# A four-layer hybrid stack on one core: x multiplied unscaled in the feed-forward stages, its transposes moved between the last row products, a shorter triangular inverse

## The reference, cut to what matters

```python
def rmsnorm(x, gain):
    y = x * lax.rsqrt(jnp.mean(x * x, axis=-1, keepdims=True) + 1e-6)
    return y * gain

def swiglu(h, w_in, w_out):                       # w_in (1024, 2*2816), w_out (2816, 1024)
    gate, up = jnp.split(h @ w_in, 2, axis=-1)
    return (jax.nn.silu(gate) * up) @ w_out

for l in range(2):                                # first block
    x = x + 0.5 * swiglu(rmsnorm(x, ffn1_norm[l]), ffn1_w_in[l], ffn1_w_out[l])
    x = x + hybrid_mixer(rmsnorm(x, mix_norm[l]), ...)
    x = x + 0.5 * swiglu(rmsnorm(x, ffn2_norm[l]), ffn2_w_in[l], ffn2_w_out[l])
for l in range(2):                                # second block
    x = x + mixer_2(rms_norm(x, g_mix[l]), ...)
    x = x + square(relu(rms_norm(x, g_ffn[l]) @ w_up[l])) @ w_down[l]   # w_up (1024, 4096)
return rms_norm(x, g_final)
```

## Time and profile before

| | |
|---|---|
| median of 3 runs | 2430.78 us (2430.58 to 2431.09) |
| the profiled execution | 2430.55 us, its span 2428.7 us |
| mean granted TensorE clock | 0.992 |
| PE busy | 2378.2 us, 98% of the span |
| DVE, ACT, POOL busy | 1549.4 (64%), 1388.8 (57%), 145.2 (6%) |
| HBM | 386.6 MB moved, 159 GB/s |

### The profile page before, as it was taken

The page is one execution under the profiler, slowest core; times in us unless marked ns, Lnnn a source line. Parts: engine busy times, 40 slices in busy tenths (PEclk is TensorE's granted clock), DMA queues, the critical chain, the costliest instruction groups (busy, mean ns, idle before and its releaser), DMA issues. The chain is left out here.

```text
span 2428.7 us, 40849 instructions
## 1 busy us (share of the span) xinstructions
PE 2378.2 (98%) x17221; PEld 2239.4 (92%) x17221; DVE 1549.4 (64%) x1891; ACT 1388.8 (57%) x1872; POOL 145.2 (6%) x119
## 2 busy tenths in 40 slices
PE   7999999999999999999999999999999999999998
PEld 7998999998999999899999899899989989998998
DVE  5555678756655655667865655559785554978545
ACT  5455788265554545678725555546854444685444
POOL 0000012100000000001300000000030000004000
PEclk9999999999999999999999999999999999999999
DMA  7554544224655555444414455544545555454553
GB/s 230 192 186 144 161 139 132 88 88 156 208 175 190 174 191 178 154 144 137 137 53 139 158 193 187 190 137 133 155 158 191 187 183 154 123 155 166 193 189 122
DMA packets 312310, 386.58 MB, mean 159 GB/s; under 512 B 10796, under 2 KB 287296, under 8 KB 312128
## 3 DMA queue, kind: packets, MB, share of 16 engines
q1 hardware_dynamic: 311848, 383.87, 48.6%
q10 hardware_dynamic: 280, 0.10, 0.0%
HBM read 382.89 MB, written 1.06 MB: 158 GB/s over the span
## 5 line engine op out<-in xcount | busy, mean ns | idle before, releaser
L275 PE MATMUL bank<-xhi,whi 128*128 128x256 f32 x3712 | 1066.7, 287 | 5.4 <-ACT xhi L383 3.4
L276 PE MATMUL bank<-xlo,whi 128*128 128x256 f32 x3712 | 1054.9, 284 | 0.0
L277 PE MATMUL bank<-xhi,wlo 128*128 128x256 f32 x3712 | 1054.8, 284 | 0.0
L267 DVE TENSOR_TENSOR wlo<-raw,whi 128x2048 fp32r<-128x2048 f32 x360 | 831.2, 2311 | 337.9 <-ACT whi L252 333.9
L252 ACT ACTIVATE whi<-raw 128x2048 fp32r<-128x2048 f32 x351 | 669.0, 1907 | 232.1 <-PE bank L277 225.4
L275 PEld LDWEIGHTS bank<-xhi,whi 128*128 128x128 f32 x3712 | 717.0, 193 | 11.6 <-issue 5.0
L276 PEld LDWEIGHTS bank<-xlo,whi 128*128 128x128 f32 x3712 | 717.0, 193 | 4.7 <-issue 1.9
L277 PEld LDWEIGHTS bank<-xhi,wlo 128*128 128x128 f32 x3712 | 716.6, 193 | 0.0
L275 PE MATMUL bank<-whi,yhi 128*128 128x512 f32 x608 | 237.5, 391 | 0.0
L276 PE MATMUL bank<-wlo,yhi 128*128 128x512 f32 x608 | 237.4, 390 | 0.0
L277 PE MATMUL bank<-whi,ylo 128*128 128x512 f32 x608 | 236.5, 389 | 0.0
(11 more groups left out here) (381 smaller groups left out, 2914.6 us busy)
## 6 DMA issues: line engine op xcount, KB each, us to landing
raw<-in_w_in SPq DMA_DIRECT2D x92, 1024.0 KB, 5.2
raw<-in_ffn_w_in SPq DMA_DIRECT2D x88, 1024.0 KB, 5.1
raw<-in_ffn_w_out SPq DMA_DIRECT2D x44, 1024.0 KB, 4.9
raw<-in_w_gate SPq DMA_DIRECT2D x32, 1024.0 KB, 5.5
raw<-in_w_up SPq DMA_DIRECT2D x32, 1024.0 KB, 5.4
raw<-in_w_down SPq DMA_DIRECT2D x32, 1024.0 KB, 4.9
raw<-in_w_branch_b SPq DMA_DIRECT2D x8, 1024.0 KB, 5.1
raw<-in_w_branch_a SPq DMA_DIRECT2D x8, 1024.0 KB, 5.2
```

Of the source, the lines that this page charges most:

```text
L267: e.tensor_tensor(wlo[s][:], raw[s][:], whi[s][:].bitcast(F32), ALU.subtract).then_inc(lo_done[s], 1)
L275: e.matmul(o, ahi, bhi, start=start, stop=False, skip_group_check=True)
L276: e.matmul(o, ahi, blo, start=False, stop=False, skip_group_check=True)
L277: return e.matmul(o, alo, bhi, start=False, stop=stop, skip_group_check=True)
```

## The change

1. Feed-forward stages (borders in `LATE_AT`: 0, 2, 3, 5, 7, 9) no longer scale x by rstd before the product. x itself is transposed, with the gain in xhi and xlo; rstd is put on a diagonal by ACT, spread over all partitions by one matmul with ones (`spread_pe`), copied by ACT (`spread_act`), and each gate and up result is multiplied by it per token: ffn1 gets two more DVE operations a block, ffn2 one operation with another operand.
2. At these borders `last_rows` runs its parts in another order, with the transposes of x by token half and column half between them (`turn_half`); the last quarter is transposed inside the first product (`late_first_product`). DVE's and ACT's norm work is ordered by column half.
3. In the delta part, POOL writes the masked blocks by column (`M_columns`); T's product at levels 4 and 5 is replaced by a transpose of U copied by ACT; level 6 works on 64 columns only.
4. The other borders keep their way; counters of semaphores are renumbered.

```diff
+        def late_first_product(e, n, o, j):
+            s, _ = n
+            def part(b, chunks):
+                for c in chunks:
+                    if b == 0:
+                        chunk_ready(e, j, c)
+                    mm = product3(...)
+                return mm
+            split_ready(e, n)
+            part(0, range(4))
+            turn_half(e, j, 1, 1)
+            part(1, range(4))
+            part(0, range(4, KC))
+            part(1, range(4, KC)).then_inc(multiplied[s], 1)
+
+        def turn_half(e, j, t, h):
+            if h and t:
+                e.wait_ge(x_new, j + 1)
+            else:
+                e.wait_ge(x_part, late(j) * 3 + (2 * h + t + 1))
+            for c in range(4 * h, 4 * h + 4):
+                late_bank = h and c == KC - 1
+                if late_bank and not t:
+                    continue
+                for u in (0, 1) if late_bank else (t,):
+                    mm = e.transpose(tq[c][:, u * P:(u + 1) * P], x[:, u, c * P:(c + 1) * P], ident)
+                if t:
+                    mm.then_inc(xt_done, 1)
+
+        def spread_pe(e, j):
+            e.wait_ge(late_norm, late(j) * 5 + DIAG_READY)
+            e.matmul(bank[1][:, 0:T], ones, diag, start=True, stop=True).then_inc(spread_product, 1)
...
+        def last_rows(e, n1, a1, n2, a2, ready2, j):
             split_ready(e, n1)
+            if j in LATE_AT:
+                row_part(e, n1, *a1, 0, 0)
+                row_part(e, n1, *a1, 1, 0)
+                row_part(e, n1, *a1, 0, 1)
+                ready2()
+                split_ready(e, n2)
+                row_part(e, n2, *a2, 0, 0, stop=True).then_inc(half_rows, 1)
+                row_part(e, n2, *a2, 1, 0, stop=True).then_inc(half_rows, 1)
+                row_part(e, n1, *a1, 1, 1).then_inc(multiplied[n1[0]], 1)
+                turn_half(e, j, 0, 0)
+                row_part(e, n2, *a2, 0, 1, stop=True).then_inc(half_rows, 1)
+                turn_half(e, j, 1, 0)
+                row_part(e, n2, *a2, 1, 1, stop=True).then_inc(multiplied[n2[0]], 1)
+                turn_half(e, j, 0, 1)
+                return
...
+        def late_border_dve(e, n, scale, j):
+            s, r = n
+            for k, (t, h) in enumerate(((0, 0), (1, 0), (0, 1))):
+                e.wait_ge(half_rows, (late(j) - 1) * 3 + (k + 1))
+                add_part(e, t, h, scale).then_inc(x_part, 1)
+            late_lo_dve(e, j, range(4))
+            e.wait_ge(multiplied[s], r + 1)
+            add_part(e, 1, 1, scale).then_inc(x_new, 1)
...
+        def late_dve(e, j, second):
+            split_lo_half(e, second, 0)
+            late_lo_dve(e, j, range(4, KC))
+            split_lo_half(e, second, 1)
+        def late_act(e, j, second):
+            split_hi(e, second)
+            late_hi_act(e, j, range(4))
+            late_square_act(e, j)
+            late_hi_act(e, j, range(4, KC))
+            late_scale_act(e, j)                 # Ln, Exp, two copies of ident scaled by rstd
...
         def ffn1_act(e, l, r0, u0, j, f):
             if first:
-                rstd_act(e, j)
+                late_square_act(e, j)
                 split_hi(e, unit(r0, u0))
                 e.wait_ge(cols_done, 1)
-                xhi_act(e, j, gain)
+                late_hi_act(e, j, range(KC))
                 split_hi(e, unit(r0, u0 + 1))
+                late_scale_act(e, j)
...
+            def scale_gate(i):                   # DVE, first in block i
+                e.wait_ge(multiplied[s], r + 1)
+                if i == 0:
+                    e.wait_ge(spread_done, late(j) + 1)
+                e.tensor_tensor(two(gbuf), two(gate_of(i)[:]), spread_two(), ALU.mult).then_inc(gate_dve, 1)
...
-                e.tensor_tensor(hbuf, hbuf, up_bank(i)[:], ALU.mult).then_inc(h_done, 1)
+                e.tensor_tensor(hbuf, hbuf, up_bank(i)[:], ALU.mult).then_inc(gate_dve, 1)
+                e.wait_ge(gate_dve, n * 3 + UP_GATED)
+                e.tensor_tensor(two(hbuf), two(hbuf), spread_two(), ALU.mult).then_inc(h_done, 1)
...
             for i in range(FF1_BLOCKS):
+                scale_gate(i)
                 if i:
                     split_lo(e, unit(r0, u0 + 3 * i + 1))
                 log_sigmoid_of_gate(i)
...
-                mm = e.matmul(bank[0][:, c * BLK:(c + 1) * BLK], M_blocks[:, :, c], const("row_of"), ...)
+                mm = e.matmul(bank[0][:, c * BLK:(c + 1) * BLK], M_columns[:, c, :], const("row_of"), ...)
...
+                last = s == LEVELS - 1           # U times L, and T times M, at the last level:
+                            mm = e.matmul(b4(g)[0:64, i, 64:P], Lb[g][:, i, 0:64], Ub[g][:, i, 64:P], ...)
+                            mm = e.matmul(b4(g)[0:64, i, 0:64], Tb[g][:, i, 0:64], Mb[g][:, i, 64:P], ...)
-                            mm = e.matmul(halves(b4(4 + g)[:, i, 0:64], s, False), Mb[g][:, i, :],
-                                          halves(Tb[g][:, i, :], s, True)[:, :, 0, :], start=True, stop=True)
+                if not last:
+                    for g in range(GROUPS):
+                        e.wait_ge(*V["tu_done"](l, (s - LOW + 1) * 4 + g))
+                        for i in range(4):
+                            mm = e.transpose(b4(4 + g)[:, i, :], Ub[g][:, i, :], ident)
+                        mm.then_inc(V["t_turned"].sem, 1)
...
+            for k in range(2 * GROUPS):          # ACT
+                e.wait_ge(*V["t_turned"](l, k))
+                e.activation(flat(Tb[k % GROUPS]), bank[4 + k % GROUPS][:], ACT.Copy).then_inc(V["t_level"].sem, 1)
...
-                e.tensor_tensor(Mb[g], Lb[g], const("below")...to_broadcast([P, 4, P]), ALU.mult)   # POOL
+                e.tensor_tensor(M_columns[:, :, g * 32:(g + 1) * 32].rearrange("p c (i k) -> p i k c", i=4),
+                                Lb[g].rearrange("p i (k c) -> p i k c", c=BLK), ..., ALU.mult)
```

More of the change, by code:

```diff
@@ L235, in col, with late, normed, late_gain @@
             return cols[:, bass.ds(i, 1)] if not isinstance(i, int) else cols[:, i:i + 1]
+        LATE = (("ffn1_norm", 0), ("mix", 0), ("ffn2_norm", 0), ("ffn1_norm", 1), ("mix", 1), ("ffn2_norm", 1),
+                ("mix", 0), ("g_ffn_2", 0), ("mix", 1), ("g_ffn_2", 1), ("final", 0))
+        LATE_AT = [j for j in range(len(LATE)) if LATE[j][0] in COL]
+        NORMED_AT = [j for j in range(len(LATE)) if j not in LATE_AT]
+        ABS, EXP, LN, SIGMOID = 1, 2, 3, 4
+        SCALED, LOG_SIGMOID, UP_GATED = 1, 2, 3
+        SQUARED, LOG_TAKEN, SCALE_READY, DIAG_READY = 2, 3, 4, 5
+        def late(j):
+            return LATE_AT.index(j)
+        def normed(j):
+            return NORMED_AT.index(j)
+        def late_gain(j, c):
+            return col(*LATE[j], c)
         def unit(r0, u, i=0):
@@ new lines, in late_hi_act, with late_square_act @@
+        def late_hi_act(e, j, chunks):
+            for c in chunks:
+                e.wait_ge(xt_done, j * KC + (c + 1))
+                e.activation(xhi[:, c, :], tq[c], ACT.Copy, scale=late_gain(j, c)).then_inc(xhi_done, 1)
+        def late_square_act(e, j):
+            d = late(j)
+            e.wait_ge(x_part, d * 3 + 3)
+            e.activation(xn[:, 0, :], x[:, 0, :], ACT.Square, accum_out=sumsq[:, 0:1]).then_inc(late_norm, 1)
+            e.wait_ge(x_new, j + 1)
+            e.activation(xn[:, 1, :], x[:, 1, :], ACT.Square, accum_out=sumsq[:, 1:2]).then_inc(late_norm, 1)
@@ new lines, in late_scale_act @@
+        def late_scale_act(e, j):
+            d = late(j)
+            e.wait_ge(late_norm, d * 5 + SQUARED)
+            e.activation(lnv[:], sumsq[:, 0:2], ACT.Ln, bias=eps, scale=1.0 / D).then_inc(late_norm, 1)
+            e.wait_ge(late_norm, d * 5 + LOG_TAKEN)
+            e.activation(rstd[:], lnv[:], ACT.Exp, scale=-0.5).then_inc(late_norm, 1)
+            e.wait_ge(late_norm, d * 5 + SCALE_READY)
+            e.activation(diag[:, 0:P], ident, ACT.Copy, scale=rstd[:, 0:1])
+            e.activation(diag[:, P:T], ident, ACT.Copy, scale=rstd[:, 1:2]).then_inc(late_norm, 1)
@@ L475, in ffn1_pe @@
             first = l == 0 and u0 == 0
-            norm_pe(e, j, first)
+            if first:
+                turn_half(e, j, 0, 0)
+                turn_half(e, j, 1, 0)
+                turn_half(e, j, 0, 1)
             def gate_up(i):
@@ L2289, in ffn2_pe @@
                     e.wait_ge(*W["relu"](l, i - 2))
-                feature_product(e, up_unit(r0, u0, i), gate_of(i), xhi, xlo, j if i == 0 else None)
                 if i:
+                    feature_product(e, up_unit(r0, u0, i), gate_of(i), xhi, xlo)
                     h_ready(i - 1)
+                else:
+                    late_first_product(e, up_unit(r0, u0, i), gate_of(i), j)
+                    spread_pe(e, j)
+                if i == 1:
+                    e.wait_ge(spread_done, late(j) + 1)
                 if 0 < i < BLOCKS2 - 1:
@@ L2333, in relu @@
                     e.wait_ge(*W["square"](l, i - 1))
```

(5 more changed lines are left out.)

195 lines of the change are left out of this document (122 added, 73 removed).

## The result

The changed kernel takes 2407.91 us (median of 4 runs, 2406.05 to 2410.98) against 2430.94 us for the kernel before on the same chip (2430.58 to 2432.66): a ratio of 0.9905 [0.989, 0.992], 23.0 us faster. The forecast was 2404.3 us with a range of 2396 to 2415. The profiled execution after took 2406.55 us with a span of 2404.7; the span before was 2428.7, so the two traces differ by 24.0 us.

| term | predicted us | measured us |
|---|---|---|
| gather (its first instruction to L1300, after: L1467), two layers | -9.4 | -5.6 |
| levels, two layers | -13.0 | -15.0 |
| borders 2, 3, 5, 7, 9, without the clock | -9.2 | -11.4 |
| clock at borders 7 and 9 | -3.0 | -3.0 |
| clock elsewhere, with one wait that it had hidden before | +1.3 | +2.7 |

A forecast was written before the change was run, and what follows sets the result against it. PE, busy 98%, bounds the kernel, so gains must be PE work, idle time or clock. Terms -9.4, -13.0, -9.2, -3.0, +1.3, +2.8, +4.1 sum to -26.4 us: forecast 2404.3, range 2396 to 2415.

The forecast's parts named there:

- gather: Inverse in the delta part: contiguous loads let L1300 start 4.7 us earlier per layer, -9.4 us for two.
- levels: Inverse's three levels: T by transposes and a 64-column last level take 22.7 instead of 29.20 us, -13.0 for two layers.
- borders 2, 3, 5, 7, 9: Stage borders: transposes and spread cost PE 2.45 us instead of 4.29, 1.85 saved at each, -9.2 us.
- clock at borders 7 and 9: The two half-clock stretches after late borders vanish, 1.5 us each, -3.0 us.
- clock elsewhere: The four unchanged borders shift in time and may lose clock: 4 x 2/9 x 1.5 = +1.3 us.
- last blocks: Last block of each ffn1 stage: later split of h stalls PE 0.7 us, four times, +2.8 us.
- so 448.9: Time DVE's chain behind the gather ends; PE, ready at 447.1, waits 1.8 us before L1300.
- Rival 1: Last level: the 64-column loads give nothing, 3.2 us less gain per layer, 2410.7 us; chance 0.12.
- Rival 4: Borders: nothing removed, since xlo 4 to 7 or the diagonal come late; +9.2 us, 2413.5; chance 0.08.
- First stage: First feed-forward stage: up(0) starts 1.85 us later, rows(0) another 2.25; +4.1 us (2 to 6).
- Rivals 2: Gather: POOL's column writes are dear and the gather starts late; 2410.1 us; chance 0.12.
- rival 3: ffn1: the gate's scale delays each down unit's split, so 40 row products start late; slower, 2440 us; chance 0.04.

The follow-up runs named there:

- all_three: The changed kernel plus the edits of first_stage, last_block and pool_later together; 2395.33 us, ratio 0.9849 to the kernel before.
- split_behind: all_three with DVE's weight split between the spread and the copies before L1300 moved behind the levels; 2396.39 us, ratio 0.9856 to the kernel before.
- pool_later: The changed kernel with POOL's four q products held until DVE has spread the inverted blocks; 2406.40 us, ratio 0.9890 to the kernel before.
- last_level: The kernel before with only the last level on 64 columns, T's products kept; 2429.29 us, ratio 0.9987.
- last_block: The changed kernel, token scale before the wait for up; in ffn1's last blocks, sigmoid and gate product before the last unit's split; 2408.23 us, ratio 0.9898.
- first_stage: The changed kernel with the first stage's last transposes ahead of its first product and `setup_dve` two blocks later; 2406.60 us, ratio 0.9891 to the kernel before.

## Why the prediction was right, and where it was off

**The sum.** It came within 2.4 us of the traces' 24.0, and that is partly luck: the gather's 3.8 us, and 1.4 and 1.1 us of clock and last blocks, were lost against 4.2 us more from levels and borders.

**Gather: the mis-sized term.** Forecast 4.7 us a layer, measured 2.83 and 2.81. The part on PE's read was right: loads at 192 ns. The 3.8 us for the gather was a little high, since 3.79 / 32 took a row that runs to its modelled end: at full clock the gather takes 3.5 us to the product behind it (all_three), and with the clock falling inside it 4.05 and 4.42 after. The failing step was "The two feature products behind it take 14.27 x 0.80 = 11.4 us at full clock". They took 14.10 us at 0.80 again. The text had allowed for one fall worth 1.5 us, "inside that wait". The fall here cost 14.10 x 0.20 = 2.8 us, and the wait of 1.8 couldn't hide it: 0.83 us of it is ACT's copy of PE's own last transposes, which moves with PE and stands there after as well (`[0.83 <-ACT arena L1581]`; split_behind shows the same 0.8 with DVE out of the way). Only 1.0 was left as cover, 1.8 us went through, and 4.7 - 1.8 = 2.9 is what was measured. So the clock by itself is enough for the miss.

The rows show why half-clock time fell from 10.2 to 6.8 us in each of these stretches and the products gained nothing: before, 4.5 and 4.2 us of it lay on the gather, whose strided loads take 310 ns at either level, so the clock cost nothing there. After, 5.7 and 4.9 us lie on the products, not much less than the 5.7 and 6.0 of before, and the rest slows the contiguous gather too.

The second step, DVE's chain "so 448.9", was wrong too, hidden behind the first: it left out what POOL does to it. (Its own terms, with the overlaps that it names taken off, end at 448.4; with POOL away L1300's place comes at 18.61 us in all_three, 448.6 in the times of the trace before.) With the gather 3 us earlier, the steps begin while POOL's q products run. Before, these ended at 437.17 and the steps began at 437.49 (434.36 + 2.81, trace of before); after, they ran from 437.94 to 442.97 and the steps from 441.36. Of POOL's 5.03 us, 2 are what it loses under DVE's weight split in either kernel. pool_later and all_three show that with both costs absent the stretch is 18.6 to 18.8 us, a gain of 5.0, and the stretches of 20.0 to 20.65 us show that taking the clock's cost away alone gives back only 0.2 to 1.0: the forecast's mechanism and its sum hold under its own two assumptions.

The Trainium skill (SBUF — State Buffer, on who interferes with whom) says that a DVE instruction with two SBUF inputs contends with a GpSimd instruction that reads SBUF. The trace agrees: 1.02 us for a 0.43 us step beside POOL's products, and 2.77 us for a product of 0.73 under DVE's split. The prediction had the rows of both engines at hand, and did not put the two timelines beside each other at their new times.

**Levels: right, a little low.** 7.44 and 7.56 us a layer against 6.5. No wait came ("So nothing waits"). The last level runs at 0.060 us a step against the 0.062 worked out from the earlier trace rows. The two numbers agree by some luck, as the 0.118 it started from is 0.112 from start to start. About half of the surplus is in the last level (3.87 us instead of 4.3, without the 0.3 us hand-over that was set aside), the other half in the two levels ahead of it (17.9 us instead of 18.4). The recorded bounds don't fit each other: gains of 3.3 to 7.5 us belong to levels of 21.7 to 25.9 us, not 18.4 to 25.9. Rival 1 (64-column loads give nothing) is refuted by the step of 0.060 us. last_level adds what the prediction didn't see: without T's edit that cheaper level would have bought 1.9 us instead of 3.5.

**Borders: right, a little low.** -2.36, -2.37, -2.37, -2.18 and -2.16 us instead of 1.85 each (the half-clock stretches, 1.5 each, apart). The tight cover of 0.2 us for xlo held: there is no wait for L432 at any late border. About half of what is more than 1.85 comes from the first product itself: before, it followed its eight xlo chunk by chunk, and its 48 matmuls took 6.03 us where 48 x 0.12 = 5.76 is the pace. Those gaps of under 0.1 us are in no wait list. The rest is that transposes and spread take 2.2 us and not 2.45 (4.29 + 6.03 - 2.36 - 5.76). Rival 4 is refuted. The clock at borders 7 and 9 stayed up, worth 3.0 as said; in none of the eight traces with the new borders does it fall behind borders 2, 3, 5, 7 or 9, while the four with the old ones have one to three such falls each.

**Clock elsewhere.** The four borders that stay as they are did not lose their clock once more; the expected +1.3 came as +2.7 in other places. In layer 0 just before the gather the clock was down for 3.4 us, +1.45; before it wasn't. The other +1.27, in mix2 of layer 0, is not more time at half clock, but the same 3.4 us in a place where nothing hides it. Before, they lay between two waits of PE for DVE and shortened the second; after, PE came to the second at full speed, waited, and the clock fell behind it (PE before, then after):

```profile
1661.35 0.55 PE L1876 MATMUL bank<-table,arena 128*128 128x128 f32 x3 [0.19 <-DVE arena L2108]
```
```profile
1643.41 0.55 PE L2065 MATMUL bank<-table,arena 128*128 128x128 f32 x3 [1.83 <-DVE arena L2297]
```

A right sign for a wrong place.

**Last blocks.** 0.7 us four times was forecast; 0.87 to 0.91 came three times and 0.28 in the first of the four, 2.9 us in all against 2.8. Why the first is spared is open. The other 1.0 us is at the mixer borders 1, 4 and 6, where three of the stages end, 0.60, 0.22 and 0.13 us: there x is final later in relation to PE, and the wait at L560 is 1.64 to 1.70 instead of 1.51. last_block took the stalls (all but 0.2 us of one) and this away, so the cause is shown.

**First stage.** +1.88 for up(0), +4.3 at the last rows against 1.85 and 4.1; the wait is 2.14 us, for the split behind `setup_dve`, at 45.12 where 44.95 stood in the text. first_stage shows both causes by removing them.

**Rivals 2 and 3.** POOL's column writes cost nothing (1304 against 1288 ns), and the gather waited for no POOL. The rule of the Trainium skill that the prediction draws on (SBUF — State Buffer, on SBUF "cachelines") is borne out on PE's strided read and not on POOL's strided write; the measurement decides. In ffn1 no row product waits in mid-stage, so rival 3's 2.4 us of cover was never used up.

## What to carry to other kernels

When an edit makes one engine's step earlier, lay the timelines of DVE and POOL beside each other at their new times: two operations that used to follow one another may now overlap, and here that cost 0.6 to 2 us of a chain that was next in line. Then look whether the slow operation was slow before as well: a group's time can hold one instruction that waits for something else. A clock loss that follows a stretch of work need not go away when the stretch gets shorter, and it can move from work that it doesn't slow to work that it does; work out the chain both at 1.2 and at 2.4 GHz and see which of the two the next wait hides. Where a sum of small edits falls short, put back the parts one by one: the parts here added up to within 1 us, and the three losses pointed to a version that is 11 to 15 us faster again (11.4 by the traces, 14.5 by the medians). Where the clock scatters, a median credits an edit with what happened elsewhere; line up the starts of the same instructions instead.

## What the runs showed of the hardware

- From start to start, an fp32 step of 64 stationary and 64 moving columns runs at 0.058 to 0.060 us, with loads of 138 ns (L1475, after); 128 stationary columns with 64 moving run at 0.112 (L1311, before).
- POOL's 128x512 product with an output step of 512 bytes takes 1304 ns against 1288, while PE's load with a step of 64 bytes takes 310 against 192. The 310 ns are the same at 2.4 and at 1.2 GHz (L1283, before, 430.03 to 436.88); the contiguous load goes from 192 to 333 (L1450, after).
- DVE's chain of short steps (256 columns, then 14 to 56) with POOL's products beside its start: the 29 of them take 7.66 to 9.10 us instead of 7.06. POOL under DVE's split of 128x2048: a 128x256 product takes 2.77 to 2.82 us instead of 0.73, a 128x512 product 3.18 to 3.21 instead of 1.27, in the kernel before as well.
- Where the granted clock falls to 1.2 GHz differs between runs of one kernel. The spread of this 2.4 ms kernel, 2405.15 to 2412.46 us for the same code, goes with the mean granted clock, 0.995 to 0.992; where a fall lies matters too, since a wait behind it can hide it. A version can be told from its neighbour by 3 us only through its trace.
